# Spreading index scores and top-k between the levels of a recurrence, and lower halves of weights given to VectorE, in a four-mixer transformer kernel

## The chip, the cores and the metric

The kernel runs on one core of a Trainium2 chip. The metric is the device time of one execution in microseconds (us). A core has five engines that run their own instruction streams and wait for one another by semaphores: PE (TensorE, matrix products), DVE (VectorE), ACT (ScalarE), POOL (GpSimd) and SP (SyncE, which here only issues the weight DMAs). PE's array runs at a granted clock of 1.2 or 2.4 GHz, which the profile records as a share of full speed.

## The reference

256 tokens of width 1024 go through two stacks. In the first, each of two layers adds a mixer, an attention over a memory of 256 rows, and a product-key expert layer. The parts that the change touches:

```python
# mixer of layer 1: sparse attention beside a gated recurrence (hgrn2)
rel   = relu(einsum('bthd,bsd->bths', iq, ik) * 64**-0.5)      # index scores, 8 heads
score = einsum('bths,bth->bts', rel, iw)                       # weighed by iw
_, sel = lax.top_k(where(causal, score, -inf), 64)             # 64 keys of each token
...                                                            # softmax over sel, heads of 128
f = lb + (1 - lb) * sigmoid(f_logit); log_f = log(f); k = 1 - f
scores = einsum('bhtk,bhsk,bhtsk->bhts', q, k, decay)          # decay = exp(A_t - A_s)
# attention over the memory: keys and values of layer 1 depend on the memory alone
k, v = split(mem_n @ wkv)
# expert layer, 8 heads
s = einsum('thpd,hpnd->thpn', q, sub_keys)                     # 2 x 128 scores a head
s1, i1 = top_k(s[:, :, 0], 16); s2, i2 = top_k(s[:, :, 1], 16)
top, pos = top_k(s1[..., :, None] + s2[..., None, :], 16)      # 16 of 256 pairs
eid = i1[pos // 16] * 128 + i2[pos % 16]; g = softmax(top)
out = einsum('te,ted->td', g * gelu(einsum('td,ted->te', x, u[eid])), v[eid])
```

The second stack has latent attention, dilated attention and sliding-window attention with dense feed-forward layers. All results are float32.

## The kernel before, in words

A float32 product is made of halves: a high half rounded to the fast float32 format, and the rest as low half. Each of the 864 weight blocks (128x1024) passes one chain: SP's DMA into `ring` (two slots of two blocks), `split_high` on ACT (L536, into `wH`), `split_low` on DVE or POOL (L546, into `wL`), and on PE three matmuls for each part (L791 high by high, L792, L793). `wH` and `wL` hold NBUF = 4 blocks, so a block can be split only when PE has read the one four before it. The helper `feed(engine, n)` issues on ACT and DVE the splits that are possible by the point where PE's result number n is taken; splits stand in an engine's stream wherever `feed` is called, and are not overtaken. Which of DVE and POOL makes a block's low half is set by `pools` (L539): in either layer POOL has those from the query block `peer{l}q 8` to the expert block u42, since DVE is at work on the routing there.

PE's results go to 8 PSUM banks in the fixed order of `plan_groups`; a result waits for the reader of the one eight before. A product whose input comes late opens its first LEAD = 3 results together (`lin`, `first=`), and goes through the input's parts once, so that each part is used for three results as it arrives.

The expert layer goes through all 128 blocks of u (`acts`: PE makes 128 activations for 256 tokens, ACT applies gelu at L1461 in `acted`, and parks the result in DRAM), and then through all 128 blocks of v (`outs`: the gate, written by one-hot products `tokens`, L1009, times the activation gives the weights `gates`, L1955; their halves are `wgtH` on ACT, L1485, and `wgtL` on DVE, L1960). The order on PE in layer 0 is queries and key scores, then the layer-1 memory keys (`x1k`, 8 blocks) and values (`x1v`, 8), then u0 to u37, the transposes of the gates and indices (`slotT`), u38 to u40, and only then `tokens`, in turn with the next u blocks. Meanwhile DVE makes the routing: `top16` (L1871 to L1884) for scores of tokens 0 to 127 (tt = 0) and 128 to 255 (tt = 1), then for each tt the 256 pairs (L1910), two `top16` over them, and the look-up of the indices by comparison (L1925 to L1927, twice). In layer 1 the same is done without x1k and x1v.

In the mixer of layer 1 (odd), `odd_in` makes 30 results of the input product. The recurrence is made by `levels` 2, 4, ... 256: for each, DVE makes differences (`diff`), ACT exponentials, DVE products (`mult`, into `hg_QL`, `hg_KL`), PE scores (L1122) and DVE `keep`s them under a mask (L2190). The index scores (L1131, `scores(tt)`) and the selection of 64 keys (DVE L2243 to L2260: weighing, then 8 times maximum and replacement, for 128 and then 256 keys) follow behind the last level, before the sparse attention.

## Time and profile before

| | |
|---|---|
| runs | 2893.35, 2901.34, 2900.45 us; median 2900.45 |
| profiled execution | 2900.45 us |
| its span, first to last instruction | 2898.7 us (1.75 us lie outside) |
| mean granted clock | 0.986 |
| PE busy / idle | 2780.0 us (96%) / 118.7 |
| DVE, ACT, POOL busy | 2010.0 (69%), 1455.9 (50%), 360.0 (12%) |

An instruction's name reads output<-inputs by the program's buffers. "[x <-E buf Lnnn]" behind a row of a timeline is the idle time of the engine ahead of it, and the instruction that ended it. PEclk is in shares of 2.4 GHz. Matmul ends are modelled and overlap; the step from one start to the next is what a matmul takes: 0.12 us for 256 columns.

### The profile page before, as it was taken

The numbers are of one execution on the slowest core, as the hardware profiler recorded it, in microseconds if no ns is written. First come the engines' busy times: TensorE is split into PE (matmuls) and PEld (weight loads), VectorE is DVE, ScalarE is ACT, GpSimd is POOL, SyncE is SP. The second block draws the span as 40 slices with busy tenths as digits, with TensorE's granted clock in tenths as the row PEclk, the third lists the DMA queues.
The fourth block names the chain that finished last, engine by engine and source line by source line (L and its number), as shares of the span: only waits on it lengthen the run. The fifth ranks groups of instructions, "written<-read, shape, count | busy, mean of one in ns | idle before, by whom it ended". The sixth has DMA issues, their size and how long they took to land.

```text
span 2898.7 us, 57249 instructions
## 1 busy us (share of the span) xinstructions
PE 2780.0 (96%) x19552; PEld 2606.9 (90%) x19552; DVE 2010.0 (69%) x4363; ACT 1455.9 (50%) x2378; POOL 360.0 (12%) x208
## 2 busy tenths in 40 slices
PE   7999899999999999989999999999999999999998
PEld 6899799999988888879898999988888889999998
DVE  8557934887476777686589788657777776666765
ACT  4455344444455555455544444445555565455544
POOL 0004784000000000000179200000000000000000
PEclk9999999999999999899999999999999999999999
DMA  5445456455676665324355554566666524553454
GB/s 186 165 156 175 166 202 206 172 179 174 220 256 245 236 242 205 127 107 160 117 177 192 194 178 167 204 237 236 239 247 238 207 103 155 187 202 141 175 189 175
DMA packets 140452, 546.20 MB, mean 188 GB/s; under 512 B 15784, under 2 KB 81592, under 8 KB 83616
## 3 DMA queue, kind: packets, MB, share of 16 engines
q1 hardware_dynamic: 63216, 455.38, 44.1%
q10 hardware_dynamic: 73728, 67.14, 7.2%
q0 software_dynamic: 3376, 21.88, 2.0%
q8 instruction: 87, 1.43, 0.2%
q14 instruction: 45, 0.37, 0.0%
HBM read 505.53 MB, written 40.91 MB: 189 GB/s over the span
## 4 chain that ended last, share of the span: by engine, by line
PE 74%; DVE 9%; DMA 7%; POOL 5%; ACT 3%; issue 2%; SPq 0%; ACTq 0%; DVEq 0%
PE bank L791 22%; PE bank L793 21%; PE bank L792 21%; POOL wL L546 5%; DMA ring<-in_w_stream 4%; PE bank L1009 4%; DVE wL L546 3%; ACT wH L536 2%; DMA act_parked<-act_out 2%; PE bank L912 1%; PE bank L932 1%; PE bank L923 1%; PE bank L1122 1%; DMA x1k_parked<-x_k 0%; DVE sq L1789 0%
## 5 line engine op out<-in xcount | busy, mean ns | idle before, releaser
L546 DVE TENSOR_TENSOR wL<-ring,wH 128x1024 fp32r<-128x1024 f32 x742 | 907.2, 1225 | 619.4 <-ACT wH L536 618.1
L536 ACT ACTIVATE wH<-ring 128x1024 fp32r<-128x1024 f32 x864 | 907.0, 1055 | 403.7 <-DMA ring<-in_w_stream 203.4
L791 PE MATMUL bank<-hnH,wH 128*128 128x256 f32 x3528 | 1020.2, 289 | 34.8 <-DVE wL L546 19.1
L792 PE MATMUL bank<-hnL,wH 128*128 128x256 f32 x3528 | 1001.8, 284 | 0.0
L793 PE MATMUL bank<-hnH,wL 128*128 128x256 f32 x3528 | 1001.8, 284 | 0.0
L791 PEld LDWEIGHTS bank<-hnH,wH 128*128 128x128 f32 x3528 | 679.9, 193 | 45.3 <-issue 21.8
L792 PEld LDWEIGHTS bank<-hnL,wH 128*128 128x128 f32 x3528 | 680.3, 193 | 0.9 <-issue 0.5
L793 PEld LDWEIGHTS bank<-hnH,wL 128*128 128x128 f32 x3528 | 679.4, 193 | 0.0
L791 PE MATMUL bank<-wH,wgtH 128*128 128x512 f32 x1024 | 400.1, 391 | 4.7 <-issue 4.5
L793 PE MATMUL bank<-wH,wgtL 128*128 128x512 f32 x1024 | 399.7, 390 | 0.0
L792 PE MATMUL bank<-wL,wgtH 128*128 128x512 f32 x1024 | 399.5, 390 | 0.0
L546 POOL TENSOR_TENSOR wL<-ring,wH 128x1024 fp32r<-128x1024 f32 x122 | 324.4, 2681 | 116.8 <-ACT wH L536 72.5
L1461 ACT ACTIVATE act_out<-bank 128x256 f32<-128x256 f32 x256 | 97.7, 382 | 403.1 <-PE bank L793 339.1
L1485 ACT ACTIVATE wgtH<-gates 128x256 fp32r (+1 forms) x256 | 107.0, 418 | 257.4 <-PE bank L793 257.1
L791 PEld LDWEIGHTS bank<-wH,wgtH 128*128 128x128 f32 x1024 | 192.9, 188 | 45.3 <-issue 5.5
L793 PEld LDWEIGHTS bank<-wH,wgtL 128*128 128x128 f32 x1024 | 192.9, 188 | 40.6
L792 PEld LDWEIGHTS bank<-wL,wgtH 128*128 128x128 f32 x1024 | 193.0, 189 | 40.2
L1947 DVE TENSOR_SCALAR onehot<-con,slotT 128x128 f32<-128x128 f32 x512 | 182.5, 356 | 0.0
L1946 DVE TENSOR_SCALAR onehot<-con,slotT 128x128 f32<-128x128 f32 x512 | 146.3, 286 | 19.0 <-ACT slotT L1502 19.0
L1009 PE MATMUL bank<-onehot 128*128 128x128 f32 x1024 | 135.3, 275 | 5.5 <-DVE onehot L1947 5.5
L1009 PEld LDWEIGHTS bank<-onehot 128*128 128x128 f32 x1024 | 125.7, 192 | 5.9 <-DVE onehot L1947 5.9
L1960 DVE TENSOR_TENSOR wgtL<-gates,wgtH 128x256 fp32r<-128x256 f32 x256 | 107.8, 421 | 15.9 <-ACT wgtH L1485 14.5
(416 smaller groups left out, 3577.8 us busy)
## 6 DMA issues: line engine op xcount, KB each, us to landing
ring<-in_w_stream SPq DMA_DIRECT2D x432, 1024.0 KB, 4.9
act_parked<-act_out ACTq DMA_DIRECT2D x256, 128.0 KB, 3.6
act_in<-act_parked ACTq DMA_DIRECT2D x256, 128.0 KB, 2.7
sw_bias<-in_c_swa POOLq DMA_DIRECT2D x1, 4096.0 KB, 15.5
relb_rows<-rel_table POOLq DMA_DIRECT2D x1, 2048.0 KB, 11.3
h_parked<-h POOLq DMA_DIRECT2D x2, 1024.0 KB, 7.4
h_back<-h_parked POOLq DMA_DIRECT2D x2, 1024.0 KB, 6.4
od_relb<-relb_rows POOLq DMA_DIRECT2D x2, 1024.0 KB, 7.5
```

Of the source, the lines that this page charges most:

```text
L536: eng.activation(wH[:, b % NBUF, :], raw(b), ACT.Copy).then_inc(w_high, 1)
L546: eng.tensor_tensor(wL[:, b % NBUF, :], raw(b), wH[:, b % NBUF, :].bitcast(F32), ALU.subtract).then_inc(w_low, 1)
L791: pe.matmul(dst, lh, rh, start=start, stop=False, skip_group_check=True)
L792: pe.matmul(dst, lh, rl, start=False, stop=False, skip_group_check=True)
L793: return pe.matmul(dst, ll, rh, start=False, stop=stop, skip_group_check=True)
L912: last = pe.matmul(ps[:, 0:span], qs[c][:, tt * P:(tt + 1) * P], ks[c][:, 0:span], start=(c == 0), stop=(c == len(qs) - 1))
L1009: last = pe.matmul(psacc[j][:, m * P:(m + 1) * P], onehot[:, k, :], onehot[:, 8 + k, :], start=True, stop=True)
L1461: act.activation(act_out[:, c % 2, :], psum[c % BANKS][:, 0:T], ACT.Gelu_apprx_tanh).then_inc(u_read, 1)
L1485: act.activation(wgtH[:, c % 2, :].unsqueeze(1), gates[:, bass.ds(i * 4 + c, 1), :], ACT.Copy).then_inc(wgt_high, 1)
L1946: dve.tensor_scalar(onehot[:, k, :], iota, slotT[:, 2, bass.ds(tok, 1)], None, ALU.is_equal)
L1947: last = dve.tensor_scalar(onehot[:, 8 + k, :], iota, slotT[:, 1, bass.ds(tok, 1)], slotT[:, 0, bass.ds(tok, 1)], ALU.is_equal, ALU.mult)
L1960: dve.tensor_tensor(wgtL[:, c % 2, :].unsqueeze(1), gates[:, bass.ds(i * 4 + c, 1), :], wgtH[:, c % 2, :].bitcast(F32).unsqueeze(1), ALU.s ...
```

## The change

1. The index scores of tokens 0 to 127 are made after level 4 and those of 128 to 255 after the first two `odd_in` results of the gate, in a buffer of their own (`od_rels`). DVE weighs and selects between the `keep`s and `mult`s of the levels; `od_ckvn` is computed before `hg_f`; more `feed`s stand between.
2. In layer 0, POOL's low halves end at x1k3. DVE makes those of x1k4 to x1k7, of the eight x1v and of u0 to u27, one at each of 40 places in the routing (`one_split`), and then u28 to u42. In layer 1, POOL's end at u35 instead of u42.
3. In both layers the last four `acted` of ACT, and the low halves of the last u blocks on DVE, stand behind the first two `weights_high` and `weigh`, so that the first weights of `outs` are made earlier.
4. Five output products (both memory attentions, odd mixer, latent and sliding-window attention) open two results instead of three.

```diff
 
-        pools = [range(BNO[(f"peer{l}q", 8, 0)], BNO[(f"peer{l}u", 0)] + POOLED) for l in range(2)]
+        pools = [range(BNO[("peer0q", 8, 0)], BNO[("x1k", 4, 0)]),
+                 range(BNO[("peer1q", 8, 0)], BNO[("peer1u", 0)] + AHEAD - 4)]
 
...
 
-            def lin(name, ms, src, nk=DC, per=1, width=P, first=None, ready=None, norm_of=None, parts=None):
+            def lin(name, ms, src, nk=DC, per=1, width=P, first=None, ready=None, norm_of=None, parts=None, open_groups=LEAD):
 
                 ms = list(ms)
                 parts = list(parts or range(nk))
-                lead = ms[0:LEAD] if first is not None else []
+                lead = ms[0:open_groups] if first is not None else []
                 summed = bank(("norm", norm_of)) if lead and norm_of and norm_of not in ("mix1", "mix2") else None
                 held = [bank((name, m)) for m in lead]
...
                 last.then_inc(group_done, 1)
             level(2, 4)
+            read_of(pe, ("odd_in", IK))
+            scores(0)
             gate_rows(0)
             level(8)
             gate_rows(1)
             level(16, 32)
             lin("odd_in", HG[0:2], hn)
+            scores(1)
             level(64)
             lin("odd_in", HG[2:4], hn)
-            read_of(pe, ("odd_in", IK))
-            scores(0)
...
-            scores(1)
...
             lin("odd_out", range(8), (od_yH, od_yL), first=lambda k: read_of(pe, ("yc", k)) if k < 4 else None,
-                parts=(4, 5, 6, 7, 0, 1, 2, 3))
+                parts=(4, 5, 6, 7, 0, 1, 2, 3), open_groups=2)
...
@@ -1513,12 +1513,14 @@
                         gated(i, j)
                 for j in range(4):
                     acts_back(0, j)
-                with act.Fori(0, (N_KEYS - AHEAD - T // 4) // 4) as i:
+                with act.Fori(0, (N_KEYS - AHEAD - T // 4) // 4 - 1) as i:
                     for j in range(4):
                         acted(i, AHEAD + T // 4 + j)
                 for j in range(2):
                     weights_high(0, j)
                     acts_back(0, 4 + j)
+                for c in range(N_KEYS - 4, N_KEYS):
+                    acted(0, c)
                 for c in range(1, 3):
                     weights_high(0, c + 1)
...
             read_of(act, ("odd_in", HF[3]))
             act.activation(hg_f.rearrange("p (a b) -> p a b", a=4), od_hf, ACT.Sigmoid).then_inc(hg_sig, 1)
+            feed(act, NO[("odd_in", HQ[3])])
             act.wait_ge(hg_prod, 1)
             act.activation(hg_f, hg_f, ACT.Ln).then_inc(hg_ln, 1)
             odd_in(*HQ[2:4], IQ[0])
+            feed(act, NO[("odd_in", IQ[1])])
             decays(2)
             odd_in(IQ[1])
             copy(("ckvT",), od_ckvT.rearrange("p a b -> p (a b)"))
             odd_in(IQ[2])
             decays(4)
             odd_in(IQ[3], IK)
-            feed(act, NO[("hi", 0)])
+            feed(act, NO[("level", 2, 0)])
             decays(8, 16)
+            scores(0)
             copy(("hi", 0), od_hi[:, 0, :], cols=512)
             decays(32, 64)
             copy(("hi", 1), od_hi[:, 1, :], cols=512)
-            feed(act, NO[("level", 16, 0)])
+            feed(act, NO[("level", 16, 0)], BNO[("odd_in", HG[3], 0)])
             decays(128)
-            odd_in(HG[0])
+            odd_in(*HG[0:2])
+            feed(act, NO[("is", 1, 0)])
+            scores(1)
             decays(256)
-            odd_in(*HG[1:4])
+            odd_in(*HG[2:4])
             act.wait_ge(read_by["act"], reads[0])
             act.activation(od_hg, od_hg, ACT.Silu).then_inc(silu_s, 1)
             odd_in(0, 1)
             copy(("level256",), hg_X.rearrange("p a b -> p (a b)"), cols=512)
-            scores(0)
             odd_in(2)
-            scores(1)
             for hd in range(4):
...
+
+                def one_split(goes=True):
+
+                    if l or not goes:
+                        return
+                    b = max(fed[id(dve)][0], pools[0].stop)
+                    if b < b0 + AHEAD - 2:
+                        split_low(dve, b)
+                        fed[id(dve)][0] = b + 1
+
+                def top16(vals, idx, src, work, n, between=0):
 
                     for q in range(n):
                         last = dve.max(vals[:, q, 0:8], src[:, q, :])
                     link(last)
+                    one_split(between > 1)
...
+                            one_split(between > 0)
                     link(last)
+                    one_split(between > 1)
                     for q in range(n):
                         last = dve.max(vals[:, q, 8:16], work[:, q, :])
                     link(last)
+                    one_split(between > 0)
                     for q in range(n):
                         last = dve.max_index(idx[:, q, 8:16], vals[:, q, 8:16], work[:, q, :])
                     link(last)
+                    one_split(between > 0)
...
@@ -1923,9 +1943,14 @@
                     ranks = iota[:, 0:KTOP].unsqueeze(1).unsqueeze(1).broadcast_to([P, 8, KTOP, KTOP])
                     for s, (pos, dst) in enumerate(((pr_paf, pr_i1[tt]), (pr_pbf, pr_i2[tt]))):
                         link(dve.tensor_tensor(eq, spread(pos, 3, KTOP), ranks, ALU.is_equal))
+                        one_split()
                         link(dve.tensor_tensor(eq, eq, spread(ix[:, :, s, :], 2, KTOP), ALU.mult))
+                        one_split()
                         link(dve.tensor_reduce(dst, eq, AX.X, ALU.add))
+                        one_split()
                 feed(dve, NO[(p + "slotT", 0)])
+                for b in range(max(fed[id(dve)][0], pools[l].stop), b0 + AHEAD - 2):
+                    split_low(dve, b)
                 for tt in range(NT):
                     dve.wait_ge(exps, NT * l + tt + 1)
                     link(dve.tensor_reduce(small[:, 32:40], pr_e[tt], AX.X, ALU.add))
@@ -1933,8 +1958,9 @@
                     dve.tensor_tensor(pr_g[tt], pr_e[tt], spread(small[:, 40:48], 2, KTOP),
                                       ALU.mult).then_inc(picks, 1)
                     dve.wait_ge(picks, NT * l + tt + 1)
-                read_of(dve, (p + "slotT", 1))
-                b0 = BNO[(p + "u", 0)]
+                for b in range(b0 + AHEAD - 2, b0 + AHEAD + 2):
+                    split_low(dve, b)
+                read_of(dve, (p + "slotT", 1), feeding=False)
 
                 def rows(i, j):
...
                 for j in range(4):
                     rows(0, j)
+                    if j == 0:
+                        split_low(dve, b0 + POOLED - 1)
                     split_low(dve, b0 + POOLED + j)
                 with dve.Fori(1, T // 16) as i:
                     for j in range(4):
                         rows(i, j)
                         split_low(dve, b0 + POOLED + j, i)
-                with dve.Fori(0, (N_KEYS - AHEAD - T // 4) // 4) as i:
+                with dve.Fori(0, (N_KEYS - AHEAD - T // 4) // 4 - 1) as i:
                     for j in range(4):
                         split_low(dve, b0 + POOLED + T // 4 + j, i)
                 dve.wait_ge(g_read, (l + 1) * T // 4)
                 for j in range(2):
                     weigh(0, j)
                 weights_low(0, 0)
+                for b in range(b0 + N_KEYS - 1, b0 + N_KEYS + 3):
+                    split_low(dve, b)
                 with dve.Fori(0, N_KEYS // 4 - 1) as i:
                     for j in range(4):
...
             dve.wait_ge(odd_in_s, 32)
+            feed(dve, NO[("odd_in", HQ[2])])
+            read_of(dve, ("ckv_sq",))
+            link(dve.reciprocal(od_rel[:, 0, :], od_rel[:, 0, :]))
+            dve.scalar_tensor_tensor(od_ckvn, od_ckv, V("odd_kv_norm", 0), od_rel[:, 0, :], ALU.mult,
...
+                sc = od_sc[:, tt, 0:(tt + 1) * P]
+                best = small[:, 64 + 8 * tt:72 + 8 * tt]
+                for k in range(n):
+                    link(dve.max(best, sc))
+                    link(dve.match_replace(sc, best, sc, GONE))
+
+            def chosen(tt):
+
+                sc, sel, neg = [b[:, tt, 0:(tt + 1) * P] for b in (od_sc, od_sel, od_neg)]
...
             diff(32)
             mult(16)
+            weighed(0)
+            eights(0, 3)
             keep(8)
             diff(64)
             mult(32)
-            keep(16)
+            eights(0, 5)
+            chosen(0)
+            feed(dve, NO[("level", 16, 0)], BNO[("odd_in", HG[3], 0)])
+            keep(16, feeding=False)
             diff(128)
+            keep(32, feeding=False)
             mult(64)
-            keep(32)
+            feed(dve, NO[("odd_in", HG[1])])
+            dve.wait_ge(hg_prod, LEVELS.index(64) + 1)
             diff(256)
             mult(128)
+            weighed(1)
             keep(64)
             mult(256)
+            eights(1, 3)
             keep(128)
+            for k in range(5):
+                eights(1, 1)
+                if k == 2:
+                    feed(dve, NO[("odd_in", 2)])
+            chosen(1)
 
             def outputs_by_root():
```

The three other `lin` calls take `open_groups=2` in the same way. `split_low`, `take` and `filled` are unchanged but for the flag that skips the `feed`.

On DVE, in the look-up of the first routing for tokens 0 to 127, the stream before was:

```order
L1925 TENSOR_TENSOR pr_eq<-pr_m,con 128x2048
L1926 TENSOR_TENSOR pr_eq<-pr_eq,pr_if 128x2048
L1927 TENSOR_REDUCE pr_m<-pr_eq 128x128
L1925 TENSOR_TENSOR pr_eq<-pr_m,con 128x2048
L1926 TENSOR_TENSOR pr_eq<-pr_eq,pr_if 128x2048
L1927 TENSOR_REDUCE pr_m<-pr_eq 128x128
```

and is now (`pr_eq` holds the comparisons, L546 is a block's low half):

```order
L1945 TENSOR_TENSOR pr_eq<-pr_m,con 128x2048
L546 TENSOR_TENSOR wL<-ring,wH 128x1024
L1947 TENSOR_TENSOR pr_eq<-pr_eq,pr_if 128x2048
L546 TENSOR_TENSOR wL<-ring,wH 128x1024
L1949 TENSOR_REDUCE pr_m<-pr_eq 128x128
L546 TENSOR_TENSOR wL<-ring,wH 128x1024
L1945 TENSOR_TENSOR pr_eq<-pr_m,con 128x2048
L546 TENSOR_TENSOR wL<-ring,wH 128x1024
```

One low half stands behind every step; before, none stood there, and POOL made them beside it.

On DVE, between the levels' `keep`s (COPY_PREDICATED), before:

```order
L2190 COPY_PREDICATED hg_S<-hg_mask,bank 128x512 x2
L2164 TENSOR_TENSOR hg_dq<-hg_A 128x512
L2165 TENSOR_TENSOR hg_dk<-hg_A 128x512
L2180 TENSOR_TENSOR hg_QL<-hg_dq,od_hq 128x32x16
L2182 TENSOR_TENSOR hg_KL<-hg_dk,od_hf 128x32x16
L546 TENSOR_TENSOR wL<-ring,wH 128x1024 x4
L2190 COPY_PREDICATED hg_S<-hg_mask,bank 128x512 x2
L2164 TENSOR_TENSOR hg_dq<-hg_A 128x512
L2165 TENSOR_TENSOR hg_dk<-hg_A 128x512
L2180 TENSOR_TENSOR hg_QL<-hg_dq,od_hq 128x16x32
L2182 TENSOR_TENSOR hg_KL<-hg_dk,od_hf 128x16x32
```

The same place now, from the last of the selection of tokens 0 to 127 (`od_sel`):

```order
L2250 TENSOR_TENSOR od_sel<-od_sel,od_neg 128x128
L546 TENSOR_TENSOR wL<-ring,wH 128x1024 x3
L2220 COPY_PREDICATED hg_S<-hg_mask,bank 128x512 x2
L2194 TENSOR_TENSOR hg_dq<-hg_A 128x512
L2195 TENSOR_TENSOR hg_dk<-hg_A 128x512
L2220 COPY_PREDICATED hg_S<-hg_mask,bank 128x512 x2
L2210 TENSOR_TENSOR hg_QL<-hg_dq,od_hq 128x16x32
L2212 TENSOR_TENSOR hg_KL<-hg_dk,od_hf 128x16x32
L546 TENSOR_TENSOR wL<-ring,wH 128x1024 x2
L2188 COPY hg_dq<-hg_A 128x512
```

The fourth block's low half now stands behind the `mult` of level 64 (L2210 and L2212 with 128x16x32); the whole selection of tokens 0 to 127 stands ahead of the three that are left.

On PE the index scores of tokens 128 to 255 (L1131) now stand ahead of level 64 (L1122):

```order
@@ -3263,4 +3264,5 @@
 L792 MATMUL bank<-hnL,wH 128x256
 L793 MATMUL bank<-hnH,wL 128x256
+L1131 MATMUL bank<-od_ik,od_iq 128x256 x8
 L1122 MATMUL bank<-hg_QL,hg_KL 128x128 x8
 L791 MATMUL bank<-hnH,wH 128x256
```

The matmuls of the scores are the same, earlier in the stream; the blocks behind them keep their order.

## Rows read from the trace of the kernel before

**Rows 1.** The page: busy time, share and count of each engine.

```profile
PE 2780.0 (96%) x19552; PEld 2606.9 (90%) x19552; DVE 2010.0 (69%) x4363; ACT 1455.9 (50%) x2378; POOL 360.0 (12%) x208
```

**Rows 2.** Waits of PE, whole span: us in total, times, longest.

```profile
PE bank L791 <- DVE wL L546: 30.8, 20, 4.2
PE bank L791 <- POOL wL L546: 24.2, 19, 5.0
PE bank L791 <- issue: 6.4, 5, 2.2
PE bank L1009 <- DVE onehot L1947: 5.5, 2, 3.3
PE bank L1122 <- DVE hg_KL L2182: 4.6, 1, 4.6
PE bank L923 <- ACT att_P L1399: 3.6, 1, 3.6
PE bank L1198 <- DVE hg_f L2229: 2.6, 1, 2.6
```

**Rows 3.** Waits of PE from 284.6 to 477.8 us, the first routing.

```profile
PE bank L791 <- POOL wL L546: 17.5, 12, 5.0
```

**Rows 4.** Busy time by stretch: start:end, length, engines (instructions), PEclk, DMA share, GB/s.

```profile
284.66:389.70 105.04, 88.47 (x603) 80.80 (x603) 103.18 (x281) 38.16 (x54) 85.77 (x40) 0.97 0.49 170
345.00:400.00 55.00, 50.03 (x404) 48.79 (x403) 44.05 (x76) 23.17 (x34) 48.54 (x19) 1.00 0.60 205
1200.00:1280.00 80.00, 72.78 (x512) 69.42 (x512) 53.98 (x104) 34.99 (x62) 1.79 (x2) 0.90 0.30 106
```

**Rows 5.** PE's timeline where `outs` begins in layer 0.

```profile
788.15 0.47 PE L791 MATMUL bank<-wH,wgtH 128*128 128x512 f32 x1 [2.23 <-issue]
...
790.32 0.63 PE L791 MATMUL bank<-wH,wgtH 128*128 128x512 f32 x1
790.75 0.63 PE L792 MATMUL bank<-wL,wgtH 128*128 128x512 f32 x1
...
793.26 0.39 PE L791 MATMUL bank<-wH,wgtH 128*128 128x512 f32 x1
793.49 0.39 PE L792 MATMUL bank<-wL,wgtH 128*128 128x512 f32 x1
```

**Rows 6.** DVE's timeline in the levels: three splits in one row.

```profile
1227.19 3.50 DVE L546 TENSOR_TENSOR wL<-ring,wH 128x1024 fp32r<-128x1024 f32 x3 [3.78 <-ACT wH L536]
```

**Rows 7.** DVE's groups, 284.66 to 389.7: count | busy us, mean ns | idle.

```profile
L1926 DVE TENSOR_TENSOR pr_eq<-pr_eq,pr_if 128x2048 f32<-128x2048 f32 x4 | 15.3, 3833 | 0.1
L1925 DVE TENSOR_TENSOR pr_eq<-pr_m,con 128x2048 f32<-128x2048 f32 x4 | 11.3, 2817 | 0.1
L1927 DVE TENSOR_REDUCE pr_m<-pr_eq 128x128 f32<-128x2048 f32 x4 | 9.1, 2286 | 0.1
L1910 DVE TENSOR_TENSOR pr_c<-pr_v 128x2048 f32<-128x2048 f32 x2 | 6.6, 3318 | 0.1
L1919 DVE TENSOR_SCALAR pr_m<-pr_m 128x128 uint32<-128x128 uint32 x2 | 2.7, 1332 | 0.0
```

**Rows 8.** DVE's timeline in the first routing: start, duration in us.

```profile
323.92 0.22 DVE L1919 TENSOR_SCALAR pr_m<-pr_m 128x128 uint32<-128x128 uint32 x1
...
366.57 2.44 DVE L1919 TENSOR_SCALAR pr_m<-pr_m 128x128 uint32<-128x128 uint32 x1
```

**Rows 9.** POOL's timeline: alone, and beside DVE's comparisons.

```profile
370.50 26.10 POOL L546 TENSOR_TENSOR wL<-ring,wH 128x1024 fp32r<-128x1024 f32 x8 [1.57 <-ACT wH L536]
398.51 4.78 POOL L546 TENSOR_TENSOR wL<-ring,wH 128x1024 fp32r<-128x1024 f32 x2 [1.92 <-ACT wH L536]
```

**Rows 10.** PE's timeline: odd mixer; the last of five waits in output products.

```profile
1183.48 0.36 PE L791 MATMUL bank<-hnH,wH 128*128 128x256 f32 x1 [3.52 <-DVE wL L546]
...
2697.49 0.39 PE L791 MATMUL bank<-hnH,wH 128*128 128x256 f32 x1 [1.35 <-DVE wL L546]
```

**Rows 11.** DVE's groups from 1255 to 1298 us: the selection's maxima.

```profile
L2250 DVE MAX8 small<-od_sc 128x8 f32<-128x128 f32 (+1 forms) x16 | 5.8, 360 | 0.5
```

More of the change, by code:

```diff
@@ L552, in build_stacks, with feed @@
         fed = {}
[L554 removed]
+        def feed(eng, n, stop=len(blocks)):
             if id(eng) not in fed:
@@ L558, in feed @@
             nxt, split, own = fed[id(eng)]
-            while nxt < len(blocks) and (nxt < NBUF or last_read(nxt - NBUF) < n):
+            while nxt < stop and (nxt < NBUF or last_read(nxt - NBUF) < n):
                 if own(nxt):
@@ L1266, in _ @@
                       lambda hd, s: sw_v[:, s, (hd // 8) * 64:(hd // 8 + 1) * 64])
-            lin("o_out", range(8), (att_OTH, att_OTL), first=turned("swa"))
+            lin("o_out", range(8), (att_OTH, att_OTL), first=turned("swa"), open_groups=2)
             ffn(1)
@@ L2188, in keep @@
                 for half in range(2):
-                    ps = take(("level", lv, half))
+                    ps = take(("level", lv, half), feeding)
                     dve.copy_predicated(hg_S[:, half * 4:half * 4 + 4, :], mask,
```

84 lines of the change are left out of this document (35 added, 49 removed).

## The prediction

> **What bounds the kernel now.** I read first the busy times, then PE's waits, then the stretches, and last the timelines of those stretches in which PE waited. PE is busy for 96% of the span [rows 1]; its idle time is 118.7 us in all (2898.7 − 2780.0), so that no reordering can give more than these and what PE loses at the lower clock. The reader is to see in the waits [rows 2] that nearly all of it is small change by many causes: POOL's low halves 24.2 us, DVE's 30.8, the one-hots 5.5, the start of the v blocks 2 x 2.23 within "issue", and single waits of 2.6 to 4.6 us in the mixer of layer 1. The next view says where: of POOL's 24.2 us, 17.5 lie in the first routing, from 284.6 to 477.8 us [rows 3]. In the stretch in which DVE makes that routing it is busy 103.2 of 105.0 us [rows 4]. Behind a longer wait PE also loses speed. The 2.23 us at 788.15 are followed by instructions of 0.63 us each, which is 1.2 GHz; later ones take 0.39 [rows 5]. The steps from one start to the next are 0.43 and 0.23 us, and the slow stretch lasted from 788.8 to 792.2, so that such a fall costs 3.4 x (1 − 0.23/0.43) = 1.6 us. The timeline shows one after every wait of over 2 us, and none after those of 1.3 us and less.
>
> **Part 2, the first routing.** It removes POOL's splits beside DVE's work, and adds 40 splits to DVE. Three in one row took 3.50 us, so one is 1.17, and 1.23 when it stands alone [rows 6]: 40 x 1.23 = 49.2 us. What leaves: L1926 took 3.83 us in the mean and L1925 2.82, where L1927 with as many elements took 2.29 [rows 7]. Beside POOL the narrow L1919 took 2.44 us, and alone 0.22 [rows 8]; its neighbours L1915 and L1918 are alike. POOL pays as well: 8 splits in 26.10 us, 3.26 each, against 2.39 alone [rows 9]. Excess on DVE: L1926 15.3 − 4 x 2.29 = 6.1; L1925 11.3 − 9.2 = 2.1; L1910 6.6 − 4.6 = 2.0; three narrow ones 3 x 2.2 = 6.6; the cast at L1906 0.8; in all 17.6. DVE stood in this from 284.66 to 389.60, 104.9 us. Now: 104.9 − 17.6 + 49.2 = 136.5, so u27, the last of the 40, is ready at 421.2.
>
> PE follows. A u block is 24 matmuls of 0.1217 us, 2.92 us. From the start of u27 stand 11 blocks to the transposes, and these (1.5 us), u38, u39 and u40 ahead of the first `tokens`: 14 x 2.92 + 1.5 = 42.4. So `tokens` begins at 463.6 instead of 476.87. The wait for the one-hot (3.3, the longest of its kind [rows 2]) is within that difference: DVE has 42 us for 14 splits and the gates. The clock fall behind it (at 478.2) goes too, 1.6. Together 14.9. I take 14.0, since about every second time a new wait of 1.6 us will meet a fall. The bounds: if no wait were new, PE would gain 17.5 + 3.3 + 3 x 1.6 = 25.6. PE's new waits inside this sum are some 11 us: 1.6 at x1k4 (DVE makes it in the first `top16`, by my placing at 298 while PE wants it at 296.4), 0.8 and 1.2 at x1v, where ACT's high halves wait for the parked keys, and in the comparisons, where DVE needs 2.29 + 1.23 = 3.5 us a block against PE's 2.92, 0.6 for each of two times six blocks, and the rest at the steps of `top16` over 256 pairs, where DVE and PE go at nearly one pace. The other bound is the loss of all cover: if the comparisons stay as slow as now, 17.6 us more on DVE, 3.6 below nothing.
>
> **Part 2, the second routing.** POOL ends at u35 and no longer splits beside the one-hots: 2.2 us (5.5 − 3.3 [rows 2]) and a fall of 1.6 are gone, 3.8. POOL's waits before them (24.2 − 17.5 = 6.7 [rows 2, 3]) stay, since the comparisons still stand beside it. Bounds 0 to 6.
>
> **Part 3, the start of the v blocks.** The wait of 2.23 us [rows 5] is the chain gelu 0.38, split 1.05, `wgtH` 0.42, `wgtL` 0.42, which began only with PE's last u block. Its first two links now stand behind the weights. Four `acted` are moved with their four DMAs each way, and these find ACT 50% idle [rows 1]; the last activations go out later, but are wanted only by c = 124 and on, hundreds of us later. Next late would be the gate's multiplication, which has a whole u block of cover. In both layers: 2 x (2.23 + 1.6) = 7.6. Bounds 0 and 7.6.
>
> **Part 4, two open results.** With three open, the fourth block's low half can't begin until PE has read the first block, which is only at the last part. The last and longest of five such waits is 1.35 us [rows 10], the timeline's others are 0.82, 0.53, 0.56 and 0.88: 4.1. With two open, the third block waits whole in its buffer, and the fourth's split has the 2.9 us of the third to hide in. What could be lost is cover at the start: two results use a part for 0.72 us instead of 1.08, so the second half of the attention's output must come 8 x 0.36 / 2 = 1.4 us earlier; its halves were there 1 us or more before need. I take 4.1, bounds 0 and 4.1.
>
> **Part 1, the odd mixer.** (a) The wait of 3.52 us at 1183.48 [rows 10] is a low half that stood in DVE's stream behind `hg_f` and `od_ckvn`; it now stands ahead. With its clock fall 5.1. (b) In the levels, 4.6 (level 64 waits for `hg_KL`) and 2.6 (the root of the outputs, behind the selection) go [rows 2], each with a fall: 10.4. The cover for 23.4 us of weighing and selection, of which the 16 maxima alone are 5.8 [rows 11], is DVE's idle time, 80 − 54.0 = 26.0 in 1200 to 1280 [rows 4]. But it isn't idle everywhere, and I place three new waits: 0.4 for banks whose reader is ACT's relu, 1.5 for the low half of the first gate block, which stands behind the selection of tokens 0 to 127 (five eights of 0.72 us), and 1.9 for scores and level 64. Half a chance of one more fall is 0.8. Net 10.4 − 3.8 − 0.8 = 5.8. Bounds: nothing new 10.4; and the 23.4 us uncovered, −13. (c) The sparse attention's first wait, 3.6 for `att_P` [rows 2], began behind low halves and roots; half of it, 1.9, goes.
>
> **Sum.** 14.0 + 3.8 + 7.6 + 4.1 + 5.1 + 5.8 + 1.9 = 42.3 us. The profiled execution took 2900.45, its span 2898.7 and 1.75 around it, and is itself the median of the runs. 2900.45 − 42.3 = 2858.
>
> **Two rules weighed.** DVE's comparisons and POOL's splits slow each other, as rows 7 to 9 show. The Trainium skill ("SBUF — State Buffer", section "SBUF: two separate sides") gives the cause: the two engines share a pair of ports by an exclusive lock, taken for whole instructions, also by a DVE operation with two SBUF inputs against a GpSimd one that reads. By that rule the 17.6 us vanish with POOL's splits and the sum stands; it is why I hold the first rival below for unlikely. Against the change speaks "TensorE: Matmul & The Clock Gate", section "HAM oscillation — how this bites in real kernels": a wait in every tile can keep the array slow all along. By that the twelve comparison blocks would run at 1.2 GHz. Between 345 and 400 PE stood still for 5.0 of 55 us, in waits of 0.4 to 1.3 us each, with a granted clock of 1.00 [rows 4], which speaks against it.
>
> **The rivals.** (A) The comparisons are slow for another reason than POOL: then u27 comes 17.6 us later and the first routing gains nothing. 42.3 − 17.6 = 24.7, 2876. For it: L1926 alone of the wide ones is nearly always slow (three of four). Against: the same L1926 took 2.29 once, while POOL waited. (B) The gain is there but new waits are twice those placed: 11 + 3.8 more, or one of parts 3 and 4 gives nothing: 42.3 − 14.8 = 27.5, 2873. For it: one late split in DVE's fixed stream holds all behind it, and ACT's high halves hang on parked keys. (C) The clock falls over the twelve comparison blocks: PE needs 5.5 us a block at the lower clock (24 x 0.1217 x 0.43/0.23) against DVE's 3.5: 12 x 1.9 = 23 us more, 2881. (D) Slower: the selection holds the levels. PE waits for `mult` of level 64 and for the gate blocks behind it; if it can't use DVE's 26 us at all, 23.4 us of waiting, and the clock falls for that and the 30 us of matmuls between, which then take 30 x 0.87 = 26 us more. Less the other gains (36.5) that is 49.4 − 36.5 = 13 us slower, 2913. It decides the sign once the levels lose more than 36.5 us. Against it: ACT's relus and DVE's parts are interleaved, and only eights of 0.72 to 0.98 us stand at one place. The change not doing what it says would be a `tokens` that still waits for the one-hots; that is in B.
>
> **How the numbers follow.** My sum 0.62, A 0.12, B 0.17, C 0.05, D 0.04. The predicted time is the sum's, 2858. The range takes the sum's own 2846 (new waits half as large, 7.4, and no clock falls) to 2868, and A and B: 2846 to 2880. A change of 0.3%, 8.7 us, is about what a measurement of this kernel can tell from none. Below 2891.7 lie the sum, A, B and C but for their tails: 0.92. Within 0.3%: tails of A to C with several at once, 0.05. Above 2909.2: D, 0.03.
>
> **What would show it.** No wait for POOL's `wL` in the first routing; L1947 (the former L1926) at 2.29 us each time; u27 at 421, slotT near 453, `tokens` near 464; PE waits for DVE's `wL` in the comparisons of about 0.6 us each with a clock near 1.0. No "issue" wait where the v blocks begin. No wait of DVE's `wL` at the end of an output product. Level 64 follows the scores with less than 2 us of waiting. It is wrong if the comparisons take over 4 us without POOL, if waits for DVE's `wL` in the first routing exceed 17 us, or if the clock between 1200 and 1280 is below 0.90 [rows 4].

## The result

The changed kernel took 2853.11 us in the median of its first 4 runs (2846.96 to 2859.68) against 2900.89 (2893.35 to 2905.13): ratio 0.9839, 95% interval 0.9805 to 0.9873. Five more runs beside 11 of the kernel before gave 0.9855 (0.9834 to 0.9875). Forecast were 2858 and faster, with 2846 to 2880 as range. The profiled execution took 2848.02 us, its span is 2846.2, so that the two profiles stand 52.4 us apart, while the medians of the first runs stand 47.8 apart and those of the later ones 38.6. By the two intervals the change is worth 37 to 57 and 36 to 48 us; the 42.3 of the forecast's sum lie within both. Why the two profiles stand further apart is part of what follows.

The page of the changed kernel gives the busy time, share and count of each engine; below it stand the waits of PE over the whole span (us in total, times, longest).

```profile
PE 2761.1 (97%) x19552; PEld 2592.7 (91%) x19552; DVE 2052.4 (72%) x4425; ACT 1456.0 (51%) x2378; POOL 197.7 (7%) x146
```

```profile
PE bank L791 <- DVE wL L546: 27.9, 28, 4.2
...
PE bank L791 <- POOL wL L546: 6.4, 7, 1.3
...
PE bank L923 <- ACT att_P L1399: 2.6, 3, 2.1
PE bank L1183 <- ACT hg_X L1362: 2.6, 1, 2.6
...
PE bank L791 <- issue: 1.7, 3, 0.7
...
PE bank L1131 <- DVE hg_S L2220: 1.3, 1, 1.3
PE bank L1122 <- ACT od_rels L1626: 1.2, 1, 1.2
```

Against [rows 2]: POOL's 24.2 us are 6.4, both one-hot waits are gone, as are those for `hg_KL` and at the root, and "issue" lost its two waits of 2.23 us. New are `hg_X`, `hg_S` and `od_rels` in the levels, 5.1 us together. DVE's `wL` waits fell little in sum, 30.8 to 27.9, but they are others: 6.3 of them are new ones in the first routing, where none were. This is the row that answers to [rows 3], for 284 to 464 us:

```profile
PE bank L791 <- DVE wL L546: 6.3, 14, 1.7
```

DVE's groups in the routing, from 284.66 to 440 us (count | busy us, mean ns | idle), answer to [rows 7]:

```profile
L1945 DVE TENSOR_TENSOR pr_eq<-pr_m,con 128x2048 f32<-128x2048 f32 x4 | 9.2, 2289 | 0.1
L1947 DVE TENSOR_TENSOR pr_eq<-pr_eq,pr_if 128x2048 f32<-128x2048 f32 x4 | 9.1, 2284 | 0.0
L1949 DVE TENSOR_REDUCE pr_m<-pr_eq 128x128 f32<-128x2048 f32 x4 | 9.1, 2278 | 0.0
...
L1929 DVE TENSOR_TENSOR pr_c<-pr_v 128x2048 f32<-128x2048 f32 x2 | 4.6, 2294 | 0.1
...
L1939 DVE TENSOR_SCALAR pr_m<-pr_m 128x128 uint32<-128x128 uint32 x2 | 0.4, 222 | 0.0
```

All four comparisons take 2.28 us, the narrow operation 0.22. In layer 1 of the same execution POOL still splits beside them, and there the same line reads, in DVE's timeline (start, duration):

```profile
1487.29 4.39 DVE L1947 TENSOR_TENSOR pr_eq<-pr_eq,pr_if 128x2048 f32<-128x2048 f32 x1
```

Where the time came from is read from PE alone, since its instructions are the same in the same order, but for the index scores and the first results of the five output products: the start of one and the same matmul in both profiles. The lead of the changed kernel, in us:

| up to | lead | gained there | forecast |
|---|---|---|---|
| before the first memory keys | −0.4 | −0.4 | 0.8 (first output product) |
| behind the first `tokens` | 19.5 | 19.9 | 14.0 |
| behind the start of v, layer 0 | 23.6 | 4.1 | 3.8 |
| behind the odd mixer and its output product | 35.5 | 11.9 | 12.8 + 0.5 |
| second memory attention and its output | 36.4 | 0.9 | 0.6 |
| queries and key scores of layer 1 | 41.5 | 5.1 | 0 |
| behind the second `tokens` | 45.9 | 4.4 | 3.8 |
| behind the start of v, layer 1 | 50.0 | 4.1 | 3.8 |
| end | 52.4 | 2.4 | 2.2 (two output products) |

The first line is below its forecast since the even mixer ran 1.3 us longer at a lower clock; the output product's wait is gone.

Three stretches, which answer to [rows 4] (start:end, length, engines, PEclk, DMA share, GB/s):

```profile
345.00:400.00 55.00, 52.20 (x423) 50.78 (x422) 54.34 (x96) 23.94 (x38) 0.00 (x0) 1.00 0.63 217
...
1200.00:1280.00 80.00, 71.50 (x529) 65.61 (x528) 65.43 (x159) 45.90 (x104) 0.00 (x0) 0.98 0.29 106
...
1171.00:1250.00 79.00, 73.21 (x513) 68.95 (x514) 64.05 (x131) 33.72 (x62) 1.79 (x2) 0.92 0.32 112
```

In the first, DVE is busy for 54.3 of 55 us and so sets the pace, with PE's clock at full. The second has the same times as the row of before, but not the same work, since the changed kernel is 26 to 35 us ahead there. The third holds the matmuls that PE did from 1200 to 1280 before: on these the selection has filled DVE from 54.0 of 80 to 64.1 of 79 us, and the clock is 0.92 instead of 0.90 (0.90 in `again` below). The 0.98 of the second row is no gain of the clock: the 10.2 us at 1.2 GHz that began at 1170.3 lie outside it, while the 13.7 us from 1198.4 on lay inside the row of before.

### The profile page after: what moved, and what is told of

It reads as the page before. It is cut to its first block, busy times and chain, and to the rows that moved or that the text cites. A ratio compares the mean times of both kernels' runs of the same rounds, so it can differ in the third digit from the quotient of the medians.

```text
span 2846.2 us, 57240 instructions
## 1 busy us (share of the span) xinstructions
PE 2761.1 (97%) x19552; PEld 2592.7 (91%) x19552; DVE 2052.4 (72%) x4425; ACT 1456.0 (51%) x2378; POOL 197.7 (7%) x146
## 4 chain that ended last, share of the span: by engine, by line
PE 79%; DVE 12%; DMA 3%; POOL 2%; ACT 2%; issue 2%; DVEq 0%; SPq 0%; ACTq 0%
PE bank L791 23%; PE bank L793 23%; PE bank L792 23%; PE bank L1009 4%; DVE wL L546 3%; DMA ring<-in_w_stream 2%; POOL wL L546 2%; PE bank L912 1%; ACT wH L535 1%; PE bank L932 1%; PE bank L923 1%; DVE sq L1791 0%; DVE pr_i L1890 0%; DVE pr_i L1901 0%; DVE pr_w L1891 0%
## 5 line engine op out<-in xcount | busy, mean ns | idle before, releaser
L546 DVE TENSOR_TENSOR wL<-ring,wH 128x1024 fp32r<-128x1024 f32 x804 | 982.7, 1224 | 634.8 <-ACT wH L535 631.9
L1973 DVE TENSOR_SCALAR onehot<-con,slotT 128x128 f32<-128x128 f32 x512 | 174.6, 341 | 0.0
L546 POOL TENSOR_TENSOR wL<-ring,wH 128x1024 fp32r<-128x1024 f32 x60 | 161.7, 2713 | 73.5 <-DVE wL L546 44.4
L1972 DVE TENSOR_SCALAR onehot<-con,slotT 128x128 f32<-128x128 f32 x512 | 143.5, 280 | 0.0
```

The costliest lines, as they stand in the source:

```text
L546: eng.tensor_tensor(wL[:, b % NBUF, :], raw(b), wH[:, b % NBUF, :].bitcast(F32), ALU.subtract).then_inc(w_low, 1)
L1972: dve.tensor_scalar(onehot[:, k, :], iota, slotT[:, 2, bass.ds(tok, 1)], None, ALU.is_equal)
L1973: last = dve.tensor_scalar(onehot[:, 8 + k, :], iota, slotT[:, 1, bass.ds(tok, 1)], slotT[:, 0, bass.ds(tok, 1)], ALU.is_equal, ALU.mult)
```

## The experiments

All times are medians. The variants ran in three groups of four, each beside runs of the kernel before (2895.16 us for the first group, 2895.63 for the next, 2899.82 for the last). Nine runs of the changed kernel lie between 2847 and 2860, so a difference of less than 4 us between two variants is read from the profiles and not from medians.

**again**: no edit.

> The changed kernel once more, for a second profile. Theory (the gain is the removed waits plus the falls of PE's clock behind them): again 2846 to 2860 us; the stretches that the change touches gain the same as in the first profile, while the 5 us gained between the second memory attention and the second routing (10.2 us at 1.2 GHz around 1475 us before, none after) come or go, since no part of the change lies there. Rival (that gain belongs to the change): it is there again, to within 1 us.

2856.58 us (2847.70 to 2857.29). The stretches (length, busy time of the engines, PEclk) tell what differs between executions. Before, changed, and again, in that order; the changed kernel is 36 to 41 us ahead in layer 1, so that the work of 1470 to 1490 before lies in 1425 to 1445 there:

```profile
280.00:295.00 15.00, 15.00 (x130) 15.00 (x129) 14.62 (x94) 6.51 (x10) 10.20 (x7) 1.00 0.40 130
...
1470.00:1490.00 20.00, 18.64 (x119) 18.43 (x118) 19.45 (x120) 8.30 (x12) 9.61 (x5) 0.74 0.36 123
```

```profile
280.00:295.00 15.00, 15.00 (x130) 15.00 (x130) 14.62 (x94) 7.19 (x11) 6.00 (x5) 1.00 0.28 107
...
1425.00:1445.00 20.00, 18.64 (x159) 18.44 (x158) 19.55 (x121) 10.79 (x15) 12.82 (x6) 1.00 0.44 159
```

```profile
280.00:295.00 15.00, 15.00 (x91) 15.00 (x90) 14.62 (x95) 4.67 (x7) 5.53 (x4) 0.66 0.27 103
...
1425.00:1445.00 20.00, 18.65 (x159) 18.45 (x158) 19.52 (x118) 9.58 (x15) 13.49 (x6) 1.00 0.46 165
```

From 280 to 295 PE was busy all the time in all three, but did 130 matmuls at a granted clock of 1.00 and 91 at 0.66. At the key scores and just behind them PE stayed at 1.2 GHz for 10.2 us in one execution and not in the other, with the same 1.35 us of waiting ahead. In layer 1 it is the same place, and there the profile before had the slow stretch (0.74 in 1470 to 1490), from 1474.8 on, and both of the changed kernel had none. So this run came out as its rival has it: the 5.1 us between the second memory attention and the second routing were there again. What speaks against the rival are the later variants, none of which touches that place and in which they come and go: over all 14 profiles the same 390 matmuls took 48.5 to 48.7 us in six, 53.3 to 53.7 in five with one slow piece, 58.0 to 58.2 in three with two. The 5.1 us are therefore taken for scatter; how often the kernel before has the slow piece is not known, as it has one profile.

The first routing of "again" shows a second thing. It lost 4.8 us ahead of the memory keys, and had gained them back at the first `tokens` (459.0 against 458.9): the changed kernel's routing is paced by DVE, and what PE loses there once DVE is at work costs nothing. What makes DVE itself late does cost: in the profile of `mixer_undone` below, ACT stood 3.4 us for a block's DMA at 269 us, DVE's next steps came 3.2 us later than in "again", and `tokens` began at 464.0, though no edit lies there.

**routing0_undone** (and the guards that keep a block from being split twice):

```diff
-        pools = [range(BNO[("peer0q", 8, 0)], BNO[("x1k", 4, 0)]),
+        pools = [range(BNO[("peer0q", 8, 0)], BNO[("peer0u", 0)] + POOLED),
```

> The changed kernel with the first routing as before: POOL makes the low halves from query block 8 to u42 in layer 0, DVE none beside the routing. Theory (the ports shared with POOL): L1947 and its like rise from 2.28 to 3.3 to 3.9 us in the mean, POOL's wL waits of 17 us and the one-hot's 3.3 are back, the first tokens begin 18 us later: 2872 (2866 to 2878). Rival (the comparisons were slow for another reason, and the gain of the stretch came from elsewhere): under 8 us slower than the changed kernel.

2875.28 us (2863.95 to 2878.72), ratio 0.9918 (0.9897 to 0.9939): 18.7 us slower than "again" beside it. DVE's groups and PE's waits in the routing:

```profile
L1947 DVE TENSOR_TENSOR pr_eq<-pr_eq,pr_if 128x2048 f32<-128x2048 f32 x4 | 15.3, 3836 | 0.1
L1929 DVE TENSOR_TENSOR pr_c<-pr_v 128x2048 f32<-128x2048 f32 x2 | 12.7, 6351 | 0.1
```

```profile
PE bank L791 <- POOL wL L546: 13.3, 11, 4.4
PE bank L1009 <- DVE onehot L1974: 3.3, 1, 3.3
```

The theory holds: the comparisons are back at 3.8 us, the one-hot waits its 3.3, and from one matmul in the even mixer (at 91 us in the profile before) to another among the first of `tokens` this profile needs as long as the kernel before, 386.9 and 387.1 us; the two of the changed kernel need 367.3 and 367.5. Of the 38.6 us between "again" and the kernel before beside it, this edit alone is 19.

**mixer_undone**: the hunks of part 1 taken back (PE's; those of ACT and DVE go with them).

```diff
-            scores(0)
             gate_rows(0)
...
-            scores(1)
             level(64)
...
+            read_of(pe, ("odd_in", IK))
+            scores(0)
             lin("odd_in", [2], hn)
+            scores(1)
```

> The changed kernel with the odd mixer in the order of before (index scores and selection behind the last level). Theory: 3.5 us in front of the ninth block, 4.6 at level 64, 2.6 at the root and about 1.5 at the attention are back with their clock falls, and hg_X 2.6, hg_S 1.3 and od_rels 1.2 are gone: 12 us slower, 2865 (2860 to 2870). Rival (the new waits give back most of it): 2855 to 2859.

2866.14 us (2858.10 to 2870.62), ratio 0.9889 (0.9868 to 0.9910), 9.6 us slower than "again". In its waits (lines one higher) those of [rows 2] are back:

```profile
PE bank L1123 <- DVE hg_KL L2213: 4.6, 1, 4.6
...
PE bank L924 <- ACT att_P L1400: 2.5, 1, 2.5
...
PE bank L1199 <- DVE hg_f L2260: 2.2, 1, 2.2
```

The stretch from the layer's first block to the end of its output product took 185.8 us, against 173.7 and 175.7; in six profiles whose edits lie elsewhere it took 170.9 to 174.7, by where the clock fell. The part is worth 10 to 15 us by the profiles and 9.6 by the medians, and the forecast, 12.8, is not to be told from either.

**first_weights_undone**: the last four `acted` and DVE's last four low halves back ahead of the weights.

```diff
-                with act.Fori(0, (N_KEYS - AHEAD - T // 4) // 4 - 1) as i:
+                with act.Fori(0, (N_KEYS - AHEAD - T // 4) // 4) as i:
...
-                for c in range(N_KEYS - 4, N_KEYS):
-                    acted(0, c)
```

> The changed kernel with the last four activations and low halves again ahead of the first expert weights, in both layers. Theory: a wait of 2.2 us on PE and a fall of the clock at each start of the v blocks: 2 x 3.9 = 7.8 us slower, 2861 (2857 to 2865). Rival (the chain is hidden by the other changes, or the DMAs of the parked activations set the start anyway): within 2 us of the changed kernel.

2858.35 us (2850.91 to 2864.84), ratio 0.9874 (0.9854 to 0.9894); 1.8 us slower than "again" and 5.2 slower than the first median of the changed kernel, which settles nothing. PE's timeline at both starts does:

```profile
767.10 0.47 PE L791 MATMUL bank<-wH,wgtH 128*128 128x512 f32 x1 [2.23 <-issue]
767.41 0.39 PE L792 MATMUL bank<-wL,wgtH 128*128 128x512 f32 x1
...
769.94 0.39 PE L791 MATMUL bank<-wH,wgtH 128*128 128x512 f32 x1
...
1878.14 0.47 PE L791 MATMUL bank<-wH,wgtH 128*128 128x512 f32 x1 [2.23 <-issue]
...
1880.33 0.63 PE L791 MATMUL bank<-wH,wgtH 128*128 128x512 f32 x1
1880.76 0.63 PE L792 MATMUL bank<-wL,wgtH 128*128 128x512 f32 x1
```

Both waits are back at 2.23 us, exactly as before. Behind the first the clock stays (0.39 us an instruction), behind the second it falls (0.63). Between the same two matmuls the u blocks and the start of v take 317.7 instead of 315.3 us in layer 0, and 308.0 instead of 304.0 in layer 1. So the part is worth 2.4 or 4.0 us a layer, by whether a fall follows, and no run shows what decides that; the rival, in both its forms, is out.

**three_open, one_open**: `open_groups=3` (by leaving it out) and `open_groups=1` in the five products.

> The changed kernel with three open results in the five output products. Theory: the five waits for the fourth block's low half (0.5 to 1.4 us each) are back: 4 us slower, about 2859; in the profile each of the five products has its wait again, and nothing else differs but falls of the clock. Rival (the waits were made by DVE being late for other reasons): fewer than three of the five come back, within 2 us of the changed kernel.

> The changed kernel with one open result instead of two. Theory: the low halves need no more room than with two, while half of the cover for the second half of the input (0.36 us of matmuls for each part instead of 0.72) is gone: PE waits up to 1.4 us at the middle of each of the five products, 3 to 5 us slower than with two, 2858. Rival (fewer open results are better still, since what counts is only the block's buffer): as fast as with two or 1 to 2 us faster.

2853.45 us (2852.27 to 2859.67; ratio 0.9865, 0.9840 to 0.9891) and 2856.05 (2847.17 to 2862.25; 0.9868, 0.9842 to 0.9893): no difference that the medians could show. In the profile of three_open all five waits are back (0.70, 1.23, 0.54, 0.79, and in the last product two):

```profile
1311.50 0.39 PE L791 MATMUL bank<-hnH,wH 128*128 128x256 f32 x1 [1.23 <-DVE wL L546]
...
2647.93 0.39 PE L791 MATMUL bank<-hnH,wH 128*128 128x256 f32 x1 [0.81 <-DVE wL L546]
2650.13 0.58 PE L791 MATMUL bank<-hnH,wH 128*128 128x256 f32 x1 [1.58 <-DVE wL L546]
```

5.7 us of waits, where the changed kernel has none: the forecast 4.1 is confirmed in kind, and was 1.6 us too low, 1.0 of it in the last product. With one open, the waits at the middle of the products are there, but tiny:

```profile
PE bank L791 <- DVE att_OTL L1745: 1.3, 5, 0.3
```

0.3 us each instead of the 1.4 feared. The cover that the second result gave was not needed, and both expectations on one_open were too coarse.

**routing1_undone**: `POOLED` in place of `AHEAD - 4` for layer 1, with the same guards.

> The changed kernel with POOL's low halves of layer 1 up to u42 again. Theory: POOL's splits stand beside the one-hots of the first tokens again: a wait of 2.2 us for the one-hot, and a fall of the clock in about half of the executions: 2.2 to 3.8 us slower than the changed kernel, some 2857. POOL's own waits between the first and the last u blocks stay at 6.4 us in both. Rival (DVE, which now has six more low halves there, makes up for it): no wait for the one-hot, or 3 us of new waits for DVE's wL in the changed kernel.

2853.43 us (2850.51 to 2857.96), not to be told from the changed kernel. The profile has the wait and behind it a fall of the clock at 1575 us:

```profile
PE bank L791 <- POOL wL L546: 7.2, 7, 1.7
...
PE bank L1009 <- DVE onehot L1974: 2.6, 1, 2.6
```

The stretch from the key scores to the tokens took 127.7 us against 121.9 and 123.6. That is 4.1 to 5.8 us more, the way of the theory and above its 2.2 to 3.8, though the median doesn't show it.

**pool_to_x1k5**: POOL ends at x1k5.

```diff
-        pools = [range(BNO[("peer0q", 8, 0)], BNO[("x1k", 4, 0)]),
+        pools = [range(BNO[("peer0q", 8, 0)], BNO[("x1k", 6, 0)]),
```

> The changed kernel with POOL's low halves in layer 0 ending at x1k5 instead of x1k3. Theory: DVE's maxima are not slowed by POOL (0.41 to 0.42 us beside it and alone), so POOL can make two more low halves there for nothing; the wait of 1.7 us at x1k4 goes, DVE's places begin two blocks later and its last one is u29 at the same time, so the waits of 0.3 us in the comparisons shrink too: 2 to 5 us faster, 2850. Rival (ACT's high halves and the ring, not the low halves, hold the memory keys): the wait stays or moves to x1k6, no change.

2850.73 us (2844.30 to 2854.78), ratio 0.9848 (0.9826 to 0.9869). PE has no wait at x1k4, but neither has "again": of the profiles with this change only the two whose clock didn't fall at 280 us have it (1.69 in the changed kernel, 1.67 in first_weights_undone), so it was not worth removing. And the stretch to the one-hots is 0.9 to 1.1 us longer (368.4 against 367.5 and 367.3). DVE's timeline shows its first place in the routing:

```profile
303.57 1.23 DVE L546 TENSOR_TENSOR wL<-ring,wH 128x1024 fp32r<-128x1024 f32 x1 [6.62 <-ACT wH L535]
```

DVE stood 6.6 us for the high half of x1k6. ACT had itself stood 3.60 us ahead of it, and what ended that was the DMA that parks a memory key (`x1k_parked<-x_k`). Everything in DVE's stream, 6.6 us late, then paces PE. The theory was wrong: I counted DVE's work and not when its first piece can begin.

**x1k5_two_places_less**: the same, and DVE leaves out its first two places.

> As pool_to_x1k5, but DVE leaves out the first two of its 40 places. Theory: what spoilt that run was the first place at 297 us, where DVE stood 6.6 us for a high half that came at 303.5; with two places less in front, x1k6 is split at its third place at 302 to 304, DVE's chain is two low halves (2.3 us) shorter than in the changed kernel, and the first tokens begin at 456.5 to 457.5 instead of 459: 2 us faster, 2852. Rival (DVE's pace against PE in the first top16 decides, not the start): tokens at 459 to 460 again.

2848.35 us (2844.45 to 2849.37), ratio 0.9828 (0.9807 to 0.9848): the lowest median of all. `tokens` begin at 457.2 us, within what was expected, but mostly for another reason: this profile reached the routing 1.5 us earlier by its clock at the start. Measured from there, it is 367.2 us against 367.3 and 367.5, a gain of 0.2 and not of 2.3. DVE still stood at its first place:

```profile
300.84 1.23 DVE L546 TENSOR_TENSOR wL<-ring,wH 128x1024 fp32r<-128x1024 f32 x1 [2.06 <-ACT wH L535]
```

The 2.1 us are what the two low halves less had saved.

**level256_copy_first**:

```diff
-            copy(("level256",), hg_X.rearrange("p a b -> p (a b)"), cols=512)
+            copy(("level256",), hg_X.rearrange("p a b -> p (a b)"), cols=512, feeding=False)
```

> The changed kernel, but ACT copies level 256 (hg_X) out of PSUM before it makes the next block's high half. Theory: PE's wait of 2.6 to 3.4 us for hg_X is only the copy standing in ACT's stream behind a high half whose block is still on its way (ACT waited 4.3 us for the DMA); copied first, the wait is under 0.5 us, and the stretch of the odd mixer 2.5 us shorter, since the block is used only later: 2851. Rival (PE would wait for the late block itself a few matmuls later): the wait moves to wL behind it and nothing is gained.

2850.05 us (2843.24 to 2855.92), ratio 0.9838 (0.9814 to 0.9861). The wait for `hg_X` is gone from PE's list. ACT's timeline in the changed kernel, and then here:

```profile
1232.89 1.06 ACT L535 ACTIVATE wH<-ring 128x1024 fp32r<-128x1024 f32 x1 [4.32 <-DMA ring<-in_w_stream]
1233.85 0.58 ACT L1362 ACTIVATE hg_X<-bank 128x512 f32<-128x512 f32 x1
```

```profile
1226.90 0.60 ACT L1362 ACTIVATE hg_X<-bank 128x512 f32<-128x512 f32 x1 [0.51 <-PE bank L1173]
1231.36 1.06 ACT L535 ACTIVATE wH<-ring 128x1024 fp32r<-128x1024 f32 x1 [3.86 <-DMA ring<-in_w_stream]
```

The copy comes 7 us earlier and the block when it came before. The mixer's stretch took 170.1 us against 173.7, but it took 170.9 in two variants that leave the mixer alone, by where the clock fell, so it proves little. The piece around the wait does: from one matmul at 1223.2 us of the changed kernel's profile to another at 1252.5 it took 29.3 us, 29.4 to 29.8 in the five other profiles with this mixer that also ran 3.4 us of it at 1.2 GHz, and 27.2 here. So some 2.1 to 2.6 us are the edit's. A wait of 0.68 us for `sq` behind it is what is late next.

**layer1_by_dve**: POOL ends at u20 in layer 1, and `one_split` goes there too, for tokens 128 to 255 (shown without that second hunk).

```diff
-                 range(BNO[("peer1q", 8, 0)], BNO[("peer1u", 0)] + AHEAD - 4)]
+                 range(BNO[("peer1q", 8, 0)], BNO[("peer1u", 0)] + 21)]
```

> The changed kernel with the same recipe in layer 1 for the second half of the routing: POOL ends at u20, DVE makes u21 to u37 one at each of the 17 places of tokens 128 to 255. Theory (ports): the comparisons there fall from 4.4 to 2.3 us and the narrow ones by 2 us, 17 us in all, against 17 low halves of 1.15, 19.6; DVE's end moves by 3 us, PE waits 3 us for u21, and 4 us of POOL's waits go: 1 us faster to 2 us slower, since here no 16 blocks of memory keys give DVE time. Rival (what helped in layer 0 helps here as well): 5 to 10 us faster.

2850.22 us (2848.47 to 2857.81), ratio 0.9837 (0.9818 to 0.9857). PE's waits in the routing (1445 to 1570 us), here and in "again":

```profile
PE bank L791 <- DVE wL L546: 2.5, 6, 0.9
PE bank L791 <- POOL wL L546: 1.7, 2, 1.2
```

```profile
PE bank L791 <- POOL wL L546: 7.8, 8, 1.5
```

The stretch is 119.9 us instead of 121.9 and 123.6. That is 2.0 to 3.7 us, more than the theory had and less than the rival: u21 waited 0.9 us and not 3. The run also shows the slowdown and its end in one layer of one execution, in DVE's timeline:

```profile
1503.94 4.37 DVE L1950 TENSOR_TENSOR pr_eq<-pr_eq,pr_if 128x2048 f32<-128x2048 f32 x1
...
1546.03 2.28 DVE L1950 TENSOR_TENSOR pr_eq<-pr_eq,pr_if 128x2048 f32<-128x2048 f32 x1
```

The same instruction (L1947 of the changed kernel, three lines on) takes 4.37 us with POOL's splits beside it and 2.28 behind POOL's last.

**both_small_gains**: x1k5_two_places_less and level256_copy_first together.

> level256_copy_first and x1k5_two_places_less together. Theory: they lie in different stretches and add up: 4 to 5 us faster than the changed kernel, 2849, and 46 to 50 us faster than the kernel before. Rival (the gains drown in the falls of the clock, which come at other places then): within 2 us of the changed kernel, with other falls in the profile.

2850.87 us (2844.76 to 2854.25), ratio 0.9833 (0.9810 to 0.9856), 49 us faster than the kernel before beside it, and not to be told from either part. The piece around the former wait for `hg_X` took 26.9 us, so that gain is there again; the first routing took 367.4, so the other is not. The real one is smaller than the scatter by the clock.

## Why the prediction was right, and where its terms were off

- **First routing, 14.0 forecast, 19.9 measured.** The mechanism held: no POOL wait, comparisons at 2.28 us, DVE's chain setting the pace. Three sizes were off. One split costs DVE 1.14 us from start to start when something stands behind it, not the 1.23 of its busy time: 40 x 0.09 = 3.6 us, and the last of the 40 ended at 417.8, where I had 421.2. The way from there to `tokens` took 458.9 − 417.8 = 41.1 where I had 42.4: a u block is 2.88 us, which makes 0.6, and the transposes took 0.6 and not 1.5. And no fall of the clock came, for which I had taken off 0.9. PE's new waits were 6.3 us (3.1 in "again") and not 11. What no run separates is how much of the gain lies in DVE's shorter chain and how much in POOL's slower splits (3.26 us beside DVE against PE's 2.88 a block), for which PE had waited 17.5 us: the edit takes both away at once.
- **Its rival (A)** is out by routing0_undone, by layer 1 of the same execution (4.39 against 2.28 us) and by layer1_by_dve. **(C)**, the clock at 1.2 GHz through the comparisons, is out too: in the comparisons PE's waits were 0.2 to 0.5 us, and the granted clock is 1.00 from 345 to 400.
- **Start of v, 7.6 forecast, 8.2 measured** by the two profiles, 2.4 to 4.0 a layer by the experiment. The wait is certain; that a fall always follows was not. I had written that after every wait of over 2 us one comes and none after 1.3 us and less, and 767.10 shows a wait where none came. That was a misreading of the profile before, not news of the new one. PE's timeline there:

```profile
329.12 0.50 PE L791 MATMUL bank<-wH,memH 128*128 128x512 f32 x1 [2.32 <-POOL wL L546]
...
1473.54 0.33 PE L791 MATMUL bank<-wH,pr_qH 128*128 128x128 f32 x1 [1.36 <-DVE pr_qL L1743]
```

  The clock stayed at full behind the first, as it did behind 2.38 us at 128.2, and it fell for 10.2 us behind the second, which is shorter. That the terms with a fall came out near is therefore in part luck.
- **Output products, 4.1 forecast**: the five waits that are gone were 4.1 us, those of three_open are 5.7. The fear for the cover was without ground, as one_open shows.
- **Odd mixer, 12.8 forecast, 11.4 measured** (11.9 less 0.5 of the output product), 9.6 by the medians. Of the old waits three went as said; the attention's for `att_P` fell from 3.6 to 2.6 us, where I had half of it gone (and 1.9 for that half, which is 1.8). The new ones were 5.1 us and not 3.8, and they stood elsewhere: I had priced banks, a gate block and level 64 (1.2, near), and had missed `hg_X`, 2.6 us, the copy of level 256 in ACT's stream behind a block that had not landed. That is the step that failed in kind: I followed DVE through the levels and not the `feed`s of ACT.
- **Rival (D)**, the selection holding the levels, did not come: on the matmuls of 1200 to 1280 before, DVE is busy 64.1 of 79 us where it had been 54.0 of 80, so the selection went where DVE had been idle. The clock, whose fall below 0.90 there I had named as a sign of being wrong, hardly moved on this work (0.92, and 0.90 in "again").
- **Second routing, 3.8 forecast, 4.4 measured**; POOL's own waits stayed (6.7 and 6.4), as said.
- **What came by no part:** the 5.1 us in layer 1's queries. By the mean clocks PE spent 2 x (1 − 0.986) x 2898.7 = 81 us at 1.2 GHz in the profile before and 2 x (1 − 0.992) x 2846.2 = 46 in the one after. A part of it follows the waits that went; 10.2 us of it are the piece at 1474.8, and that is scatter. Without the 5.1 the profiles give 47.3, 5 us above the sum of 42.3, and the first routing alone is 5.9 above its term. The medians give 47.8 and 38.6 in two groups of runs, so that 2858 was as near as the scatter allows to tell.

## What to carry to other kernels

Where two engines slow each other, the work of the slower one may be nearly free on the other: here 40 low halves cost DVE 46 us and gave back 18 of its own time, and the rest lay beside matmuls of a stage that needed nothing else. Before placing work in a fixed stream, ask for each place when its input is there, since one early place holds everything behind it (6.6 us for x1k6, 2.6 for `hg_X`). And where PE's clock scatters by 5 us at the same place, compare the starts of the same matmuls in two profiles, and set aside the stretches that no edit touches.

## What the runs showed of the hardware that was not expected

- The same wait of 2.23 us ahead of the same matmuls was followed by a fall to 1.2 GHz at 1878 us and by none at 767 us in one execution.
- Without any change of the program in front of it, the stretch at 280 us ran at a granted clock of 1.00 in one profile and of 0.66 in another, 10.2 us at the lower level and 4.8 us of time. 11 of the 14 profiles have this piece. Another of 10.2 us, from 1170.3 in the changed kernel's profile, began with no wait of PE in the 9 us ahead of it.
- L1929, a wide DVE operation on two inputs, took 4.91 and 7.79 us beside POOL's splits in routing0_undone, 2.29 and 4.34 us in the profile before and 2.29 in the changed kernel, without them. What decides how much it loses is not shown. DVE's maxima and replacements over 256 elements took 0.41 to 0.42 us with POOL at work and without.
